# Attention's output products in K quarters and a rounded gather and scatter around 16 experts, in a fused two-block kernel

## The reference

```
attn = rmsnorm(heads, subln_g) * 0.8                      # norm over the 128 of each head
y    = sigmoid(ga)*(attn @ w_attn_out) + sigmoid(gf)*(four @ w_four_out)
x    = x + g1 * (y @ w_out)
h2   = rmsnorm(x)*(1 + sc2)*norm2_g + sh2                 # sc2, sh2, g1, g2 from c @ w_mod
gates = top 2 of 4 experts in the best of 4 groups, softmaxed
x    = x + g2 * sum_e gates[e] * ((silu(h2 @ w1[e]) * (h2 @ w3[e])) @ w2[e])     # 16 experts
out  = rmsnorm(x) * final_g
```

## Time and profile before

| | us |
|---|---|
| three runs | 1125.32, 1128.25, 1122.80 |
| median | 1125.32 |
| the profiled execution's own time | 1122.61 |
| its span in the trace | 1120.8 |
| PE busy in it | 1022.1 (91%) |
| DVE, ACT, POOL busy | 480.6, 408.7, 389.7 |
| transfers | 246.60 MB, mean 220 GB/s |

### The profile page before, as it was taken

The page is one execution under the profiler, slowest core; times in us unless marked ns, Lnnn a source line. Parts: engine busy times, 40 slices in busy tenths (PEclk is TensorE's granted clock), DMA queues, the critical chain, the costliest instruction groups (busy, mean ns, idle before and its releaser), DMA issues.

```text
span 1120.8 us, 13844 instructions
## 1 busy us (share of the span) xinstructions
PE 1022.1 (91%) x5577; PEld 745.7 (67%) x5577; DVE 480.6 (43%) x628; ACT 408.7 (36%) x600; POOL 389.7 (35%) x191
## 2 busy tenths in 40 slices
PE   3998799967999999998899989996989999999994
PEld 3997687745899988987698856664766434444331
DVE  4468322371355435545407417774454122222224
ACT  4444754512554344333454425553233211111001
POOL 4579573833730000002587834446640000000000
PEclk9999899998899999998899999998998999999997
DMA  9545342655665665756254532235687799999960
GB/s 319 189 148 186 112 159 73 218 186 208 199 205 177 237 225 159 261 183 224 80 184 150 188 99 89 75 113 186 253 300 295 298 421 421 422 420 422 420 256 39
DMA packets 84515, 246.60 MB, mean 220 GB/s; under 512 B 4388, under 2 KB 8123, under 8 KB 72031
## 3 DMA queue, kind: packets, MB, share of 16 engines
q1 hardware_dynamic: 82766, 240.47, 58.8%
q0 software_dynamic: 1264, 2.41, 0.9%
q10 hardware_dynamic: 416, 2.77, 0.6%
HBM read 244.59 MB, written 1.05 MB: 219 GB/s over the span
## 4 chain that ended last, share of the span: by engine, by line
PE 80%; DVE 9%; ACT 4%; issue 2%; DMA 2%; POOL 2%; SPq 0%; POOLq 0%; ACTq 0%; DVEq 0%
PE gemm_ps L1217 10%; PE gemm_ps L758 8%; PE gemm_ps L759 7%; PE gemm_ps L760 7%; PE gemm_ps L762 7%; PE gemm_ps L764 7%; PE gemm_ps L763 7%; PE gemm_ps L1248 5%; PE mix_ps L1258 2%; PE gemm_ps L1201 2%; PE mix_ps L758 2%; PE mix_ps L759 2%; PE mix_ps L760 2%; PE gemm_ps L936 1%; DMA ring<-in_w_out_dram 1%
## 5 line engine op out<-in xcount | busy, mean ns | idle before, releaser
L442 POOL TENSOR_TENSOR w_lo<-ring,w_hi 128x1024 fp32r<-128x1024 f32 (+1 forms) x144 | 360.1, 2523 | 423.0 <-ACT w_hi L436 422.9
L436 ACT ACTIVATE w_hi<-ring 128x1024 fp32r<-128x1024 f32 (+2 forms) x222 | 227.2, 1035 | 295.8 <-PE gemm_ps L764 97.1
L758 PE MATMUL gemm_ps<-w_hi,acts 128*128 128x512 f32 (+2 forms) x448 | 179.3, 400 | 27.1 <-POOL w_lo L442 10.4
L762 PE MATMUL gemm_ps<-acts,w_hi 128*128 128x256 f32 x640 | 184.9, 289 | 3.8 <-DVE acts L1729 2.4
L764 PE MATMUL gemm_ps<-acts,w_lo 128*128 128x256 f32 x640 | 181.8, 284 | 0.0
L763 PE MATMUL gemm_ps<-acts,w_hi 128*128 128x256 f32 x640 | 181.7, 284 | 0.0
L759 PE MATMUL gemm_ps<-w_lo,acts 128*128 128x512 f32 (+2 forms) x448 | 174.4, 389 | 0.0
L760 PE MATMUL gemm_ps<-w_hi,acts 128*128 128x512 f32 (+2 forms) x448 | 173.8, 388 | 0.0
L442 DVE TENSOR_TENSOR w_lo<-ring,w_hi 128x1024 fp32r<-128x1024 f32 (+1 forms) x78 | 90.7, 1170 | 107.5 <-ACT w_hi L436 107.3
L762 PEld LDWEIGHTS gemm_ps<-acts,w_hi 128*128 128x128 f32 x640 | 123.5, 193 | 9.3 <-issue 6.5
L763 PEld LDWEIGHTS gemm_ps<-acts,w_hi 128*128 128x128 f32 x640 | 123.5, 193 | 1.3 <-issue 1.2
(11 more groups left out here) (347 smaller groups left out, 1423.9 us busy)
## 6 DMA issues: line engine op xcount, KB each, us to landing
ring<-in_w_in_dram SPq DMA_DIRECT2D x56, 1024.0 KB, 5.2
ring<-in_w_mod_dram SPq DMA_DIRECT2D x24, 1024.0 KB, 5.2
ring<-in_w_ffn_in_dram SPq DMA_DIRECT2D x20, 1024.0 KB, 5.2
late_ring<-in_w_exp_down_dram SPq DMA_DIRECT2D x20, 1024.0 KB, 12.4
late_ring<-in_w_exp_gate_dram SPq DMA_DIRECT2D x18, 1024.0 KB, 12.7
late_ring<-in_w_exp_up_dram SPq DMA_DIRECT2D x18, 1024.0 KB, 10.5
ring<-in_w_ffn_out_dram SPq DMA_DIRECT2D x11, 1024.0 KB, 9.4
ring<-in_w_exp_up_dram SPq DMA_DIRECT2D x9, 1024.0 KB, 11.5
```

The lines of the kernel that those rows point to most:

```text
L436: nc.scalar.activation(part(w_hi, u), raw_unit(u), ACT.Copy).then_inc(hi_made, 1)
L442: eng.tensor_tensor(part(w_lo, u), raw_unit(u), part(w_hi, u), ALU.subtract).then_inc(lo_made[unit["maker"]], 1)
L758: mm(dst, xh, wh, start=a_, stop=False, skip_group_check=True)
L762: mm(dst, wh, xh, start=a_, stop=False, skip_group_check=True)
```

## The change

Four edits in one.

1. `ao` and `out2` become four products each by K half and column half: `ao_a` (K tiles 0 to 3, both column halves), then `ao_b` (K tiles 4 to 7). The accumulation stays in the same PSUM banks. `turn` becomes `half_turn`, and the first half of `cols` is a function of its own, so a product of the first K half needs only half of the turned tokens.
2. The heads' norm is taken in two parts. Part one (heads 0 to 3): variance after step n = 12 on DVE, the power on POOL after the rest of `g2`'s unit 13, the products on DVE after n = 14. Part two after the last head.
3. The gather takes x as a rounded part `XH` (ACT) plus a rest `x_low` (DVE), both fp32r, and a PICK in fp32r; the scatter takes YS as rounded plus rest, and a PICK_T in fp32r. PICK has three buffers instead of two, PICK_T one instead of two, YS one pair instead of two.
4. The gates are no longer folded into PICK. `slot_gates` gathers them into the slots (four small fp32 matmuls a group), and the YS copies multiply by them.

```
-    out += [("ao", cols(a["w_attn_out_2"][0], COL * h)) for h in range(2)]
+    quarters = [("a", 0, 0), ("a", 0, 1), ("b", COL, 0), ("b", COL, 1)]
+    out += [("ao_" + part, cols(a["w_attn_out_2"][0, k:k + COL], COL * h)) for part, k, h in quarters]
...
-    out += [("out2", cols(a["w_out_2"][0], COL * h)) for h in range(2)]
+    out += [("out2_" + part, cols(a["w_out_2"][0, k:k + COL], COL * h)) for part, k, h in quarters]
... SP: load_first
-                if c == index["ao"][0]:
+                if c == index["ao_a"][1]:
                     sp.wait_ge(sem("heads_made"), HEADS2 * TT)
...
-                elif c == index["out2"][0]:
-                    sp.wait_ge(*last_product(index["ao"][1]))
+                elif c == index["out2_a"][0]:
+                    sp.wait_ge(*last_product(index["ao_b"][1]))
                     for slot in after_ao:
                         load_late(FIRST + slot)
... POOL
-            lo_up_to(end_of("g2"))
+            lo_up_to(units_of[index["g2"][3]][1])
+            root(ds[:, 32:40])
             lo_up_to(end_of("fo"))
-            root(ds[:, 32:48])
+            root(ds[:, 40:48])
... PE
+            def half_turn(name, src, rows_sem, half):
+                pe.wait_ge(sem(rows_sem), TT * (half + 1))
+                for b in (2 * half, 2 * half + 1):
+                    for k in (2 * b, 2 * b + 1):
+                        for t in range(TT):
+                            last = nc.tensor.transpose(turned_to(name, k)[:, t * P:(t + 1) * P], src[:, t, k * P:(k + 1) * P], ident)
+                    last.then_inc(turned, 1)
...
+            pe.wait_ge(sem("probs"), 2 * N)
+            half_turn("heads", O, "heads_normed", 0)
+            fo_unit(2)
             fo_unit(3)
+            half_turn("heads", O, "heads_normed", 1)
             pe.wait_ge(sem("silu_E"), 1)
             mod_rows("mod_g1", 0)
...
+            pe.wait_ge(cols_dve, 2 * TURN["heads"] + 1)
             for half in range(2):
+                pair_free_wait(pe, y0 + 3 + half)
+                quarter("ao", 0, half, y0 + 3 + half, 0)
+                if half == 0:
+                    mod_spread("mod_g1", 0)
+            pe.wait_ge(cols_dve, 2 * TURN["heads"] + 2)
+            quarter("ao", 1, 0, y0 + 3, 0)
+            quarter("ao", 1, 1, y0 + 4, 0, after_unit=[lambda: (mod_rows("mod_g1", 1, 0, KT // 2), half_turn("y2", Y, "y_rows", 0))])
             mod_rows("mod_g1", 1, KT // 2, KT)
+            pe.wait_ge(cols_dve, 2 * TURN["y2"] + 1)
+            pair_free_wait(pe, step["out2"])
+            quarter("out2", 0, 0, step["out2"], 1)
+            mod_spread("mod_g1", 1)
+            half_turn("y2", Y, "y_rows", 1)
... (router's bias)
+            pair_free_wait(pe, step["out2"] + 1)
+            quarter("out2", 0, 1, step["out2"] + 1, 1)
...
+            pe.wait_ge(cols_dve, 2 * TURN["y2"] + 2)
+            quarter("out2", 1, 0, step["out2"], 1)
+            quarter("out2", 1, 1, step["out2"] + 1, 1, after_unit=[lambda: (mod_rows("mod_g2", 0, 0, KT // 2), x4_first())])
... ACT
+            cols("heads", 0, HEADS_T, scale=lambda k: feat("subln_g_2"))
             gate_row(0)
+            hi_up_to(units_of[index["out2_a"][1]][-1])
+            gate_row(1)
             cols("y2", 1, Y_T, scale=lambda k: 0.5)
-            gate_row(1)
-            hi_for("out2", 1)
+            hi_up_to(units_of[index["out2_b"][1]][-1])
... DVE
+                if n == 12:
+                    heads_var(0)
+                if n == 14:
+                    heads_scaled(0)
... experts, PE
-                        last = mm(dst[...], XN3[:, t, k * P:(k + 1) * P], PICK[:, g % 2, t, :], ...)
+                for v in parts:                       # XH, x_low
+                            last = mm(dst[...], v[:, t, k * P:(k + 1) * P], PICK[:, g % 3, t, :], ...)
...
             for q in range(4):
-                gather(0, q)
+                if q == 2:
+                    pe.wait_ge(sem("totals_read"), 1)
+                gather(0, q, (XH,))
             mod_spread("mod_g2", 1)
+            for q in range(4):
+                pe.wait_ge(sem("x_low"), 2 * (q // 2 + 1))
+                gather(0, q, (x_low,))
...
+                if s < NEXP and s % PER_GROUP == 0:
+                    slot_gates(s // PER_GROUP)
...
-                if s >= 3:
-                    scatter((s - 3) // 2, (s + 1) % 2)
+                if s >= 3 and s % 2 == 1:
+                    for t in range(TT):
+                        scatter((s - 3) // 2, t)
... scatter: two fp32r products (rounded, rest) for one fp32 product; ACT and DVE, for each half:
+                        A(YS[r:r + WIN, 0, half, :], DOWN[b, :], ACT.Copy, scale=SLOT_GATES[r:r + WIN, e:e + 1]).then_inc(sem("y_high"), 1)
+                        V_.scalar_tensor_tensor(YS[rows_, 1, half, :], DOWN[half * WIN:(half + 1) * WIN, :], SLOT_GATES[rows_, e:e + 1],
+                                                YS[rows_, 0, half, :], ALU.mult, ALU.subtract).then_inc(sem("y_low"), 1)
... DVE, after pick_rows(0): four x_low = x * root - XH of 128x512, then the totals; pick_gates (five operations a pair) is gone
```

More of the change, by code:

```diff
@@ L204, in plan_units @@
             counts[unit["maker"]] += 1
-            if u != of_chunk[unit["chunk"]][-1] and chunks[unit["chunk"]][0] != "branch":
+            if chunks[unit["chunk"]][0] in ("ao_a", "out2_a") or u != of_chunk[unit["chunk"]][-1] and chunks[unit["chunk"]][0] != "branch":
                 unit["used"] = counts["used"]
@@ L764, in product_unit @@
                             last = mm(dst, wl, xh, start=False, stop=b_, skip_group_check=True)
-                    if at_end and n:
+                    if at_end and n and "used" not in unit:
                         last.then_inc(s, n)
-                if not at_end:
+                if "used" in unit:
                     last.then_inc(sem("unit_used"), 1)
@@ L1121, in _, with quarter @@
+            def quarter(name, kh, half, p, r, after_unit=()):
+                product(index[name + ("_a", "_b")[kh]][half], rows(p, lambda t: tokens(r, t, k0=4 * kh)),
+                        first=(kh == 0), final=(kh == 1), after_unit=after_unit)
+            pe.wait_ge(sem("probs"), 2 * N)
+            half_turn("heads", O, "heads_normed", 0)
+            fo_unit(2)
             fo_unit(3)
+            half_turn("heads", O, "heads_normed", 1)
             pe.wait_ge(sem("silu_E"), 1)
             mod_rows("mod_g1", 0)
-            turn("heads", O)
@@ L1125, in _ @@
-            cols_ready("heads")
+            pe.wait_ge(cols_dve, 2 * TURN["heads"] + 1)
             for half in range(2):
-                pair_free_wait(pe, step["y"] + 3 + half)
-                product(index["ao"][half], rows(step["y"] + 3 + half, lambda t: tokens(0, t)),
-                        after_unit=[lambda: None, lambda: mod_spread("mod_g1", 0)] if half == 0 else ())
-            mod_rows("mod_g1", 1, 0, KT // 2)
-            turn("y2", Y)
-            mod_rows("mod_g1", 1, KT // 2, KT)
@@ L1162, in logits_first @@
                 logits(0, 4)
-            for half in range(2):
-                pair_free_wait(pe, step["out2"] + half)
-                product(index["out2"][half], rows(step["out2"] + half, lambda t: tokens(1, t)),
-                        after_unit=[lambda: mod_spread("mod_g1", 1)] if half == 0 else [lambda: None, x4_first, logits_first])
-            mod_rows("mod_g2", 0)
+            pe.wait_ge(cols_dve, 2 * TURN["y2"] + 2)
+            quarter("out2", 1, 0, step["out2"], 1)
+            quarter("out2", 1, 1, step["out2"] + 1, 1, after_unit=[lambda: (mod_rows("mod_g2", 0, 0, KT // 2), x4_first())])
+            logits_first()
+            mod_rows("mod_g2", 0, KT // 2, KT)
             pe.wait_ge(sem("x_3"), 3)
@@ L1188, in _, with gather @@
             mod_rows("mod_g2", 1, KT // 2, KT)
[L1191 removed]
+            def gather(g, q, parts=(XH, x_low)):
                 pe.wait_ge(sem("picked"), g + 1)
[L1193 to L1196 removed]
                 dst = gathered_to(g, q)
[L1198 to L1203 removed]
+                for v in parts:
+                    for i in range(2):
+                        k = 2 * q + i
+                        for t in range(TT):
+                            last = mm(dst[:, i * GROUP_SLOTS:(i + 1) * GROUP_SLOTS], v[:, t, k * P:(k + 1) * P], PICK[:, g % 3, t, :],
+                                      start=(v is XH and i == 0 and t == 0), stop=(v is x_low and t == TT - 1), skip_group_check=True)
+                if parts[-1] is x_low:
+                    last.then_inc(sem("gathered"), 1)
             def gate_and_up(e):
```

212 lines of the change are left out of this document (117 added, 95 removed).

## The result

| | before | after |
|---|---|---|
| median of the runs, us | 1125.57 (20) | 1131.54 (20) |
| profiled execution, us | 1122.61 | 1127.78 |
| its span, us | 1120.8 | 1126.0 |
| mean granted clock in it | 0.961 | 0.955 |

The changed kernel is slower by 0.4%: the ratio of its time to the kernel before is 1.0040, 95% interval 1.0025 to 1.0055. One of its runs took 1998.96 us and is left out of the comparison. Forecast were 1108.3 and, with 0.87, a faster kernel. The profiled execution is one of its quicker ones: its granted clock was 0.955, while most of the others had 0.945 to 0.952 and took 1128 to 1134 us; where those lose more, no trace shows.

A forecast was written before the change was run, and what follows sets the result against it. PE was taken as the bound, ending last just behind a full weight stream. Expert steps -12.4, close +0.3, first gather -2.6 and attention -2.3 sum to -17.0 us: 1108.3 on the median, range 1098 to 1118.

The forecast's parts named there:

- By the same durations: `fo` ends at 778.6, part two is turned at 780.9: Attention's end: with the old kernel's durations, ao_a starts 3.0 us ahead, after 6.8 us of new costs.
- (b): Attention loop after n = 14: two DVE norm products beside POOL take about 3.4 us, all passed on to PE.
- (a): Attention loop: the first power on POOL delays `g2`'s unit 14, so PE waits 3.4 us.
- (c): Behind `ao`: the late out2_a piece, landing 9.9 us after `ao`, delays the gate row; PE idles 4.4 us.
- The first gather: Before expert 0's product: gather with its spread takes 8.2 to 9 us in all, 2.6 less; bounds -2 and 3.5.
- The expert steps: Faster gathers and scatters, less new waits and small gate products: 12.4 us less in sum; bounds 7 and 21.
- the wait of 0.89 before an even step's down product: Even steps from 4, without scatter in between: PE waits about 0.94 us for ACT to empty the shared bank.
- the last step's wait: Step s = 16: DVE's staggered YS operations take 2.1 us ahead of its copies; the step still takes 1.7 less.
- Rival 4: Expert steps: small waits lower the clock, 1.8 us lost per step; 1137 us if all 16 do; chance 0.07.
- rival 1: Expert stage: PE saves about 21 us and the weight stream ends last; 1102.1 us on the median; chance 0.17.
- The side taken as slower, 0.07: Chance of a kernel slower by more than 0.5% (5.6 us).
- Rival 3: Attention loses more: slower DVE passes, lower clock after three waits, gather at its bad bound; 8 us worse, 1116; chance 0.13.

The follow-up runs named there:

- hold_piece: `hold` with the second `out2` piece issued before the two expert pieces and the gate row's copy ahead of its rounding on ACT; 1113.46 us, ratio 0.9911.
- hold_totals: `hold` with DVE's maximum of the expert totals ahead of the four x_low operations instead of behind them; 1110.74 us, ratio 0.9884.
- hold: The changed kernel with one more wait on POOL: ao_a's roundings start only after DVE's four products of the heads' norm; 1114.23 us, ratio 0.9903.
- the three small waits together: `hold` with totals' maximum first, first root after all `g2` roundings, and early `out2` piece with gate row's copy first; 1106.86 us, ratio 0.9820.

## Why the prediction was wrong

**The step that failed** is "By the same durations: `fo` ends at 778.6, part two is turned at 780.9". Under (b) I took a DVE pass beside POOL at 2.02 us for the first half. For the second half I took the durations of the kernel before, in which the products of both halves take 2.36 us together, so about 1.3. It took 10.81. Two things were wrong. I never laid POOL's queue over the moved products: the term of the added line, four roundings ahead of the loads, isn't in the sum at all. And I took one neighbour, 2.02, for the price of an overlap, when it is the price of waiting out the rest of one rounding. The timeline of before had two rows that say so (POOL, and DVE beside it):

```profile
777.20 7.06 POOL L442 TENSOR_TENSOR w_lo<-ring,w_hi 128x1024 fp32r<-128x1024 f32 x3
...
782.11 2.71 DVE L1728 CAST acts<-arena 128x1024 fp32r<-128x1024 f32 x1
```

A cast that takes 0.69 us elsewhere began 0.2 us into the last of three roundings and ended 0.56 us after it. These rows give the price of one rounding and no more: no DVE operation of the kernel before waited for several, so its trace could have warned of an overlap, but would have put it at 2 to 3 us and not at 10. The Trainium skill has the mechanism (SBUF — State Buffer, "SBUF: two separate sides"): DVE and GpSimd share one pair of ports by an exclusive lock for a whole instruction, and a DVE operation with two SBUF inputs or in a two-port mode waits for it. By that rule the product, which began 0.4 us ahead of POOL's first rounding, would have waited for none, or at most for one, 2.3 us. The runs show that it can be passed over by four (10.2 us) and by six (15.2 us); that it is this lock that they wait for is the page's account, and no run here isolates it.

What followed: ao_a began at 796.04 instead of 783.1, and `mod_rows` behind `ao` at 823.2, with `ao` forecast to end at 810.8. `ao` itself took the 27 us that it was given. From there to the last turnings of x it was 44.1 us instead of 38.6. PE's waits in it are as long as forecast (2.84 + 1.84 against 4.4). The other 5 us fit the clock, which was 0.85 on average in these 44.1 us and stood lowest behind the second wait:

```profile
840.00:850.00 10.00, 10.00 (x41) 8.88 (x40) 3.90 (x4) 5.55 (x8) 5.04 (x3) 0.63 0.64 235
```

**(a)** was right in kind: PE waited 2.02 us for POOL (3.4 forecast) where it hadn't before, and the power took 1.65 (1.66). **(b)** for the first half was right: 3.45 us (3.4), and part of the 5.66 us before the first unit of `fo`, which waited 3.21 before. Together they made `fo` begin at 763.05 instead of 757.60, 5.5 us later, where 6.8 were taken:

```profile
742.66 10.06 POOL L455 TENSOR_TENSOR w_lo<-ring,w_hi 128x1024 fp32r<-128x1024 f32 x4
745.14 0.47 PE L772 MATMUL gemm_ps<-w_hi,acts 128*128 128x512 f32 x1 [2.02 <-POOL w_lo L455]
755.71 3.45 DVE L2058 TENSOR_TENSOR arena<-arena,st 128x512 f32<-128x512 f32 x2
763.05 0.77 PE L772 MATMUL gemm_ps<-w_hi,acts 128*128 128x512 f32 x1 [5.66 <-issue]
```

**(c)** had the piece right (9.4 us against 9.9; 810.8 + 9.9 is 820.7, not the 820.5 written) and its importance wrong: 1.84 us of idle PE, not 4.4, because PE had first stood for DVE's stalled chain, 2.84 us here and 6.65 in `hold_piece`.

**The first gather** gave nothing instead of 2.6. An x_low operation took 1.06 us, not 0.75 (the row of 0.75 has no strided operand; no run tests whether that is why), so PE waited 2.10 for the maximum behind the four, and ran at the lower clock: eight rounded products took 2.08 us, as long as the sixteen of the rest at 889.05 (2.09). With the maximum first the term comes true: in `hold_totals` the stretch is 4.1 us shorter than in `hold`.

**The expert steps** were right in sum: -11.3 against -12.4, with the wait of 0.89 before an even step's down product as foreseen, and eight such waits in all. PE's waits from 880 to 1105, by releaser (us in total, times, longest):

```profile
PE gemm_ps L1293 <- ACT arena L1683: 4.5, 5, 0.9
PE gemm_ps L1280 <- DVE arena_rounded L2247: 3.9, 3, 2.5
PE gemm_ps L1293 <- DVE arena L2262: 2.6, 3, 0.9
```

The 2.5 in the second row is the last step's wait, forecast at 2.1. Rival 4, the falling clock, occurred in one product (5.35 us at 1058.11 instead of 3.65, behind two such waits), not in ten: the clock of the stretch is 0.98. The stream stayed hidden; rival 1 didn't occur.

**The chances.** The side taken as slower, 0.07, hung on one mechanism of the expert stage. Rival 3 had attention losing 8 us and was the nearest; it had no term for a stall longer than one rounding. Even with the stall taken away by `hold` the ratio is 0.9903 against the 0.985 of the forecast; the three small waits together close that gap (0.9820).

## What to carry to other kernels

When an operation of DVE that works in SBUF is moved, lay POOL's queue over its new place and count how many POOL operations stand there in a row: the wait can last for the whole row, and it can also end after one of them, so take both as bounds. A backlog on POOL is made elsewhere (here by ACT rounding ahead), so reordering POOL's own queue moved the stall to the next DVE operation, while a wait that lets DVE go first cost nothing as long as POOL's results weren't due. Each such edit should be judged by its wait in the trace and by a combined run, since one by one they are lost in the spread.

## What the runs showed of the hardware

- A DVE operation from SBUF to SBUF beside POOL's roundings of 128x1024 (2.3 us each in a row, up to 2.96) took 10.20 us (two operands, four in a row), 10.15 (one tensor operand and a scalar a partition, four) and 15.17 (six). Others in such rows came through after one: 2.74, 2.09, 2.12. A scalar product of 128x512 in the same place took 0.92 us in seven traces and 5.57 to 5.65 in three. Operations of 128x512 with an operand in PSUM weren't held up: 0.62 to 0.69 us.
- POOL loses little by it: four roundings took 9.23 us while DVE stood, and 10.06 to 11.30 where DVE operations came through between them.
- A power of 8 columns on POOL took 1.65 us, between 0.72 for 2 and 2.91 for 16.
